# Four ring groups at first, meta indices selected earlier, and the mixer's last products dealt out in steps between the meta rows

## The reference, cut to what matters

```
h = concat(meta_tokens (16), x (512)), padded          # d = 1024
h = h + even_layer(h)      # attention + short conv, then [att, conv] @ w_out
h = h + peer_ffn(h)        # layer 0
h = h + odd_layer(h)       # pooling
h = h + peer_ffn(h)        # layer 1
return h[:, 16:528]

peer_ffn, for a block of tokens:
    hb = rms_norm(h)
    q = hb @ w_query                       # 8 heads x 2 halves x 128
    s = q . sub_keys                       # 128 scores in each of 16 lists
    sv, si = top_k(s, 16)                  # per list
    top_s, top_pos = top_k(sv0[:, None] + sv1[None, :], 16)   # per head
    idx = si0 * 128 + si1 at top_pos       # 128 experts of each token
    gate = softmax(top_s)
    act = gelu(u[idx] . hb)
    y = sum(gate * act * v[idx])           # u, v: 16384 x 1024 per layer
```

## Time and profile before

| | |
|---|---|
| time, median of 3 runs | 3064.41 us (3062.91 to 3065.80) |
| the profiled execution | 3064.01 us, its span 3062.0 us |
| busy share of the span | PE 62%, DVE 68%, ACT 24%, POOL 32% |
| chain that ended last | DMA 57%, PE 18%, DVE 13%, issue 10% |
| moved | 1140.14 MB, mean 372 GB/s; gathers 1090.59 MB |
| loads that wait for the last product (`odd_weights_sync`) | 1540 KB |

### The profile page before, as it was taken

The page is one execution under the profiler, slowest core; times in us unless marked ns, Lnnn a source line. Parts: engine busy times, 40 slices in busy tenths (PEclk is TensorE's granted clock), DMA queues, the critical chain, the costliest instruction groups (busy, mean ns, idle before and its releaser), DMA issues.

```text
span 3062.0 us, 41832 instructions
## 1 busy us (share of the span) xinstructions
PE 1902.6 (62%) x13374; PEld 782.9 (26%) x13374; DVE 2097.0 (68%) x6444; ACT 725.9 (24%) x2829; POOL 994.9 (32%) x1112
## 2 busy tenths in 40 slices
PE   9999866664756466545665566555755566545444
PEld 4765422221222122122222222221222222211111
DVE  2143568887778668676788677866877688755556
ACT  2035112222222222123222222132212322122212
POOL 0000133333443333233333333333333333333332
PEclk9999978776877678767777787777876777666666
DMA  5131389999999999999999999999999999999998
GB/s 195 56 131 55 110 335 418 407 412 420 421 419 413 409 420 408 421 413 416 413 412 411 419 413 413 410 412 421 404 416 410 419 412 407 417 419 417 417 418 336
DMA packets 165492, 1140.14 MB, mean 372 GB/s; under 512 B 18672, under 2 KB 19696, under 8 KB 29856
## 3 DMA queue, kind: packets, MB, share of 16 engines
q0 software_dynamic: 149760, 1090.59, 86.7%
q1 hardware_dynamic: 15520, 46.94, 4.1%
HBM read 1135.30 MB, written 2.10 MB: 371 GB/s over the span
## 4 chain that ended last, share of the span: by engine, by line
DMA 57%; PE 18%; DVE 13%; issue 10%; ACT 1%; POOL 0%; POOLq 0%; DVEq 0%; SPq 0%
DMA ring_early<-in_peer_uv,idx_u 21%; DMA ring_early<-in_peer_vu,idx_u 19%; DMA ring_late<-in_peer_uv,idx_u 10%; DMA ring_late<-in_peer_vu,idx_u 7%; PE psum L1550 3%; PE psum L732 3%; DVE ring_early L1674 3%; PE psum L1105 3%; PE psum L774 2%; PE psum L635 2%; DVE ring_late L1674 2%; PE psum L668 1%; DVE work L1222 1%; PE psum L1083 1%; DVE si L1220 1%
## 5 line engine op out<-in xcount | busy, mean ns | idle before, releaser
L1674 DVE SCALAR_TENSOR_TENSOR ring_early<-ring_early,psum 128x1024 f32<-128x1024 f32 x696 | 847.0, 1217 | 427.4 <-DMA ring_early<-in_peer_vu,idx_u 214.4
L1550 PE MATMUL psum<-ring_early,w_col 128*32 128x256 f32 x5472 | 530.8, 494 | 704.3 <-ACT w_col L1609 647.5
L1674 DVE SCALAR_TENSOR_TENSOR ring_late<-ring_late,psum 128x1024 f32<-128x1024 f32 x344 | 418.8, 1217 | 212.2 <-DMA ring_late<-in_peer_uv,idx_u 141.6
L1471 POOL DMA_INDIRECT ring_early<-in_peer_vu,idx_u x348 | 328.3, 943 | 596.2 <-DVE ring_early L1674 364.3
L1471 POOL DMA_INDIRECT ring_early<-in_peer_uv,idx_u x348 | 326.5, 938 | 591.3 <-DVE ring_early L1674 407.6
L1550 PE MATMUL psum<-ring_late,w_col 128*32 128x256 f32 x2720 | 270.5, 493 | 352.2 <-ACT w_col L1609 326.1
L1550 PEld LDWEIGHTS psum<-ring_early,w_col 128*32 128x32 f32 x5472 | 190.9, 132 | 1078.2 <-issue 754.0
L1609 ACT ACTIVATE w_col<-block_fold,weight 128x32 f32<-128x32 f32 x1024 | 269.3, 313 | 666.9 <-DVE weight L1651 654.3
L1605 ACT ACTIVATE ge<-ga 128x4 f32<-128x4 f32 (+1 forms) x265 | 54.4, 205 | 1321.4 <-DVE ga L1635 1321.4
L1105 PE MATMUL psum<-wq,hbT 128*128 128x512 f32 x512 | 321.5, 717 | 35.9 <-DVE work L1222 34.8
L1471 POOL DMA_INDIRECT ring_late<-in_peer_uv,idx_u x172 | 161.1, 937 | 301.4 <-DVE ring_late L1674 238.7
(11 more groups left out here) (266 smaller groups left out, 2144.1 us busy)
## 6 DMA issues: line engine op xcount, KB each, us to landing
wq<-in_peer_w_query SPq DMA_DIRECT2D x16, 1024.0 KB, 18.7
w_ring<-in_even_w_in SPq DMA_DIRECT2D x5, 2048.0 KB, 7.9
ring_early<-in_peer_vu,idx_u POOLq DMA_INDIRECT x348
ring_early<-in_peer_uv,idx_u POOLq DMA_INDIRECT x348
w_ring<-in_even_w_out SPq DMA_DIRECT2D x1, 4096.0 KB, 14.1
ring_late<-in_peer_vu,idx_u POOLq DMA_INDIRECT x172, 12.9
ring_late<-in_peer_uv,idx_u POOLq DMA_INDIRECT x172, 12.9
hT<-in_x_T SPq DMA_DIRECT2D x4, 528.0 KB, 6.9
```

Of the source, the lines that this page charges most:

```text
L1471: nc.gpsimd.indirect_dma_start(pair_cells(at), None, uv_rows if at.side else vu_rows, bass.IndirectOffsetOnAxis(idx_u[par][:, i:i + 1], 0) ...
L1550: nc.tensor.matmul(block_part(b, n), w_col[:, i % W_SLOTS, :], v_cell(at)[:, part_cols(n)], start=False, stop=last, skip_group_check=True) ...
L1674: nc.vector.scalar_tensor_tensor(out=cell, in0=cell, scalar=1.0, in1=rows, op0=ALU.mult, op1=ALU.mult, accum_out=dot[par][:, i:i + 1]).the ...
```

## The change

- `ORDER` uses the four early groups for the first 40 rows (16 meta rows and 24 of tile 0), and all six from row 40 on; `late_constants` moves on POOL's queue from behind meta row 7 to ahead of row 40.
- TensorE: product 3 moves behind the meta scores, product 4 ahead of the transposes of tile 0; the selection of indices comes before the first query. Products 5 to 9 are cut into nine steps each (`project_step`: the residual or one k) that run as hooks, two behind each meta row at first, and one behind each tile row until row 14. Fill 0 becomes a hook of row 10 and waits for `s_mix` at 5. The wait for all additions moves to tile row 14.
- PSUM banks: products 4 and 6 use bank 3, the rest bank 5; the first query uses bank 5.
- ACT: the meta queries' copies come ahead of tile 0's norm; copies of products 5 to 9 become hooks of rows 5, 9, 13, 21 and 31.
- VectorE: the addition of product 3 and tile 0's norm run inside the meta sort; tile 0's first sort runs in one piece ahead of the dots, its second between the dots of rows 2 to 14.
- The third and fourth queries move from rows 7 and 23 to 13 and 29; the first two of tile 1 from 31 and 47 to 34 and 49; several hooks of tile 0 move by a few rows.

```diff
-META_ORDER = [0, 1, 2, 3, 0, 1, 2, 3, 4, 5, 0, 1, 2, 3, 4, 5]
-EARLY_ROWS = META_ORDER.index(GROUPS_EARLY)
-ORDER = META_ORDER + [n % RING for n in range(2 * XT * TILE_ROWS)]
+EARLY_TILE_ROWS = 24
+EARLY_ROWS = CHUNK + EARLY_TILE_ROWS
+ORDER = ([n % GROUPS_EARLY for n in range(EARLY_ROWS)] +
+         [(GROUPS_EARLY + n) % RING for n in range(2 * XT * TILE_ROWS - EARLY_TILE_ROWS)])
...
         def late_bank(i):
-            return QUERY_BANK if i % 2 else LATE_BANK
+            return psum[:, 3, :] if i in (4, 6) else LATE_BANK
+
+        BANK_FREE = {4: 2, 5: 2, 6: 3, 7: 4, 8: 6, 9: 7}
...
+        PRODUCT_STEPS = 1 + KD
+        PRODUCTS_EARLY = 2 * (CHUNK - 1)
+
+        def project_step(pe, n):
+
+            i, k = 5 + n // PRODUCT_STEPS, n % PRODUCT_STEPS - 1
+            t, half = PROJECTED[i // 2], i % 2
+            c = slice(512 * half, 512 * half + 512)
+            if k < 0:
+                pe.wait_ge(s_mix, BANK_FREE[i])
+                nc.tensor.matmul(late_bank(i), ident[:, :], hres[:, t, c], start=True, stop=False)
+                return
+            ins = nc.tensor.matmul(late_bank(i), catT[:, k, cols_of(t)], w_out_sb[:, k, c], start=False, stop=(k == KD - 1))
+            if k == KD - 1:
+                ins.then_inc(s_proj, 1)
...
             if f:
                 pe.wait_ge(s_dot, CHUNK + RUN * (f - 1))
+            else:
+                pe.wait_ge(s_mix, 5)
...
-        META_QUERIED = (7, 23)
-        FIRST_QUERIED = (31, 47, 63, 79)
+        META_QUERIED = (13, 29)
+        SECOND_SORT = 2
+        FIRST_QUERIED = (34, 49, 64, 79)
...
-            gather_pool(pool, None, 0, range(EARLY_ROWS))
-            late_constants(pool)
-            gather_pool(pool, None, 0, range(EARLY_ROWS, CHUNK))
+            gather_pool(pool, None, 0)
...
+                    if j == 0 and c == EARLY_TILE_ROWS // CHUNK:
+                        rows = EARLY_TILE_ROWS % CHUNK
+                        gather_pool(pool, j, c, range(rows))
+                        late_constants(pool)
+                        gather_pool(pool, j, c, range(rows, CHUNK))
...
-            columns_scalar(act, None, 0, of_chunk(early, 0) + [(12, lambda: piece_exponentials(act, 1)), (12, lambda: stage_gates(act, 1, 1))])
+            columns_scalar(act, None, 0, [(4, first_indices), (5, lambda: piece_exponentials(act, 0)), (5, lambda: take_projected(act, 5)),
+                                          (9, lambda: take_projected(act, 6)), (12, lambda: stage_gates(act, 1, 1)),
+                                          (13, lambda: take_projected(act, 7))] +
+                           of_chunk(early, 0))
...
-            stages = topk_stages(dve, first_piece(1) + 1, 1, P)
-            dots_vector(dve, None, 0,
-                        [(1 + i, stages[i]) for i in range(TOPK_STAGES)] +
-                        [(14, lambda: piece_indices(dve, 1)), (15, lambda: piece_gates(dve, 0))])
+            first = topk_stages(dve, first_piece(1), 0, P)
+            second = topk_stages(dve, first_piece(1) + 1, 1, P)
+            meta_gates_vector(dve)
+            for stage in first:
+                stage()
+            piece_indices(dve, 0)
+            early = ([(SECOND_SORT + i, second[i]) for i in range(TOPK_STAGES)] +
+                     [(SECOND_SORT + TOPK_STAGES, lambda: piece_indices(dve, 1))] +
+                     routing_vector(dve, 1, META_QUERIED, 2, piece_indices))
+            dots_vector(dve, None, 0, of_chunk(early, 0) + [(11, lambda: piece_gates(dve, 0))])
...
             pe.wait_ge(s_setup, SETUP_STEPS)
-            pe.wait_ge(s_mix, 2 * XT)
             open_meta_sum(pe)
-            fill_tensor(pe, 0)
             early = routing_tensor(pe, 1, META_QUERIED, 2)
-            meta_sums_tensor(pe, of_chunk(early, 0) + [(CHUNK + RUN - FILL_AHEAD, lambda: fill_tensor(pe, 1))])
+            products = [(n // 2 if n < 3 * PRODUCT_STEPS else n // 2 + 1, lambda n=n: project_step(pe, n)) for n in range(PRODUCTS_EARLY)]
+            late = ([(n - PRODUCTS_EARLY, lambda n=n: project_step(pe, n)) for n in range(PRODUCTS_EARLY, 4 * PRODUCT_STEPS)] +
+                    [(6 + n, lambda n=n: project_step(pe, 4 * PRODUCT_STEPS + n)) for n in range(PRODUCT_STEPS)])
+            meta_sums_tensor(pe, products + [(10, lambda: fill_tensor(pe, 0)),
+                                             (CHUNK + RUN - FILL_AHEAD, lambda: fill_tensor(pe, 1))] + of_chunk(early, 0))
```

More of the change, by code:

```diff
@@ L1809, in _ @@
             pool.wait_ge(s_meta_rows, 1)
[L1810 to L1812 removed]
+            gather_pool(pool, None, 0)
             def tile(j):
                 for c in range(TILE_CHUNKS):
[L1816 removed]
+                    if j == 0 and c == EARLY_TILE_ROWS // CHUNK:
[3 more added lines that the diff above has]
+                        gather_pool(pool, j, c, range(rows, CHUNK))
+                    else:
+                        gather_pool(pool, j, c)
                     if j == 1 and c < len(WINDOWS):
@@ L1843, in _, with first_indices @@
             stage_u(act, 0, 0)
+            first_query(0)
             take_projected(act, 4)
-            take_projected(act, 5)
-            take_projected(act, 6)
             first_query(1)
-            act.wait_ge(s_piece, 1)
-            stage_u(act, 1, 1)
-            piece_exponentials(act, 0)
-            for i in range(7, 2 * TILES):
-                take_projected(act, i)
+            def first_indices():
+                act.wait_ge(s_piece, 1)
+                stage_u(act, 1, 1)
             def tile(j, hooks, more=True):
@@ L1904, in _ @@
             add_projected(dve, 2)
-            add_projected(dve, 3)
-            norm_vector(dve, 1, P, tile_of(0), 0)
-            for stage in topk_stages(dve, 0, 0, P, meta=True):
+            for i, stage in enumerate(topk_stages(dve, 0, 0, P, meta=True)):
+                if i == 7:
+                    add_projected(dve, 3)
+                if i == 10:
+                    norm_vector(dve, 1, P, tile_of(0), 0)
                 stage()
@@ L1911, in _ @@
             gates_vector(dve, 0, P, 2)
-            stages = topk_stages(dve, first_piece(1), 0, P)
-            for i, stage in enumerate(stages):
-                if i == 4:
-                    meta_gates_vector(dve)
-                if i == TOPK_STAGES - 1:
-                    dve.wait_ge(s_gateT, 1)
-                stage()
-            piece_indices(dve, 0)
             def tile(j, hooks):
@@ L1966, in _ @@
             first_query(0)
-            pe.wait_ge(s_routed, 2)
-            meta_select_tensor(pe, top_i, META_IDX, s_midx)
-            project_tensor(pe, 4)
-            pe.wait_ge(s_gate, 1)
-            meta_select_tensor(pe, soft, META_GATE, s_gateT)
             pe.wait_ge(s_idx, 1)
             pe.wait_ge(s_mgate, 1)
-            project_tensor(pe, 5)
-            project_tensor(pe, 6)
-            pe.wait_ge(s_mix, 4)
             first_query(1)
-            for i in range(7, 2 * TILES):
-                project_tensor(pe, i)
             def tile(j, hooks):
```

37 lines of the change are left out of this document (20 added, 17 removed).

## The result

The changed kernel takes 3077.05 us (median of six, 3070.80 to 3079.31); the kernel before, run beside it, 3063.58 us (median of six, 3062.78 to 3065.80). The ratio is 1.0040, interval 1.0030 to 1.0051: slower by 0.4%, where 3053.0 was forecast. The profiled execution took 3079.31 us around a span of 3077.6 us, so this trace stands 15.6 us behind the span of before, 2 us more than the medians do.

A forecast was written before the change was run, and what follows sets the result against it. The DMA was taken as the bound, with only waste before about 400 us winnable. Row 22 at 441.2 less (423.0 + 3.8 + 3.0) gave 11.4 us off the 3064.4 median: 3053.0, range 3042 to 3062.

The forecast's parts named there:

- What bounds the kernel: DMA is full from 400 us to 3040 us, so only DMA time wasted before about 400 us can count.
- Part 1: Indices earlier: one product fewer ahead of the meta queries, gather 0 at 333.4, 3.3 us earlier, alone worth nothing.
- Part 2: Tile 0's first sort: first dot at 358.5, 2.8 us later; VectorE's 13.38 and 15.83 us waits go.
- Part 3: Dots with the second sort between them: 2.4 us per row on VectorE, inside the DMA's 2.53, so not the bound.
- Part 4: TensorE in the meta rows: first sum 368.8, rows at 2.47 then 3.33 us, gather 22 issued 418.1, landed 423.0.
- the first rival: TensorE keeps up in the meta rows: DMA full from about 361.5, row 22 lands at 410.9, 3041; chance 0.17.
- the third rival: TensorE's clock stays low in its rows 1 to 13: 21 us more, 3074, slower; chance 0.10.
- the sum behind it: From row 22: gain 441.2 less 423.0 landing, 3.8 odd weights and 3.0 for the ring of four, 11.4 us.
- What else moves, at no cost: POOL's memset and wait, SP's odd loads, tile 1's transposes and later sorts move without costing time.
- Four gathers (10 us) are in flight when it opens: Tile 1's transposes at TensorE's row 37 wait for a sort stage at row 45; gathers in flight cover it.
- There is a little room left: Later sorts at a 15-row instead of 16-row distance fit, VectorE's busy share being about 0.9 with a full DMA.
- The second rival: Ring of four starves up to row 40: 2.8 to 2.9 us a row, about 9 us more, 3062, no change; chance 0.15.

The follow-up runs named there:

- e2: Changed kernel with the third query's last step at row 9 instead of 13, so the fourth query's wait reaches 3 rows, not 7: 3067.58 us.
- e12: Changed kernel with only gelu batches of two rows instead of four in rows 0 to 31: 3073.58 us.
- e11: e7 with gelu batches of two rows instead of four in rows 0 to 31: 3054.52 us.
- e7: e6 with TensorE's product steps dealt out more thinly, and ACT's copies of products 7 and 8 moved with them: 3060.21 us.
- e10: Kernel before with four groups for the first 40 rows, shorter waits for the fourth query and tile 1's transposes, and two-row gelu batches in rows 0 to 31: 3073.55 us.
- e13: Kernel before, six groups kept, with only gelu batches of two rows in rows 0 to 31: 3069.12 us.
- e6: Changed kernel with the third query at row 9, tile 1's queries at 31, 47, 63, 79 and its transposes at tile row 24 instead of 21: 3059.24 us.
- e1: Changed kernel with tile 1's queries back at rows 31, 47, 63, 79, 16 rows apart: 3073.14 us.
- e14: Kernel before with only tile 1's queries moved to rows 34, 49, 64, 79, 15 rows apart: 3070.71 us.
- e4: Kernel before with only four groups for the first 40 rows and the POOL wait and clearing moved ahead of row 40: 3083.63 us.
- e15: Changed kernel with third query at 9, tile 1's queries at 31, 47, 63, 79, its transposes at tile row 24, two-row gelu batches in rows 0 to 31: 3054.82 us.

## Why the prediction was wrong, by its own steps

- *What bounds the kernel*: right. The DMA is full behind 680 us at 415 GB/s in after, and every difference between the kernels was made in the gathers ahead of it.
- *Part 1*, gather 0 at 333.4: it went out at 335.12, 1.6 us earlier than before and not 3.3. The mixer ended 0.7 us later in this execution, and from the start of product 4's residual to the transposes behind it were 9.5 us (322.31 to 331.84), where 8.0 was given. Gather 0 alone was worth nothing, as forecast.
- *Part 2*, first dot at 358.5: 360.39, late by 1.9 us, about what gather 0 was late. The waits of 13.38 and 15.83 us on VectorE are gone, as forecast.
- *Part 3*, VectorE not the bound: right.
- *Part 4*, the meta rows: right in its terms up to gather 22, so the first rival (TensorE keeps up) did not come about. First sum forecast at 368.8, measured 370.87; row 0 forecast at 4.5, measured 3.96 (370.87 to 374.83); pitch 2.47 and 3.33 forecast, 2.47 (374.83 to 377.30) and 3.33 (398.86 to 402.19) measured; row 15's sum at 420.54; gather 22 forecast at 418.1, measured 420.42, 2.3 us late, most of it gather 0's delay of 1.7. Its row's dot ran at 425.88, where 423.0 was forecast for the landing. Granted clock 0.65 in 360 to 380, with 15.70 us of idleness ahead of the first sum, and 1.00 from 380 to 420, which is 2.4 GHz: the third rival, a low clock, did not come about, and the slower result has another cause.
- *The step that failed* is the end of part 4 and the sum behind it: "afterwards TensorE has one step a row, 1.6 to 2.0 us, and the DMA is full again", with "Bounds: 0 ... and 18 x 0.25 plus 1.5 for a late stage, 6 us. I take 3." At row 22 the changed kernel's dot was 15.4 us ahead of before, where 18.2 was forecast. Behind row 22 the sum allowed a loss of 6.8 us (3.8 for the weights, 3.0 for the ring), and the dots lost 31.3 by row 200. Rows 22 to 29 of TensorE also hold the fourth query, and its first step waits for a stage seven rows later on VectorE; the sum has no term for that but the 1.5 us for a late stage. In the rows of before such a wait is harmless, because six groups are in use. A ring of four lets a gather go eight rows behind its sum, so a reach of 7 leaves the DMA one or two rows: 10.9 us, shown by shortening that reach (e2). And I had priced the ring by its rate with four in flight, not by the loop of gelu batch, sum and gather, which is eight rows long as well: 4.3 us in the changed kernel (e12), 5.5 with the waits gone (e11 less e7), about 9 as an estimate with four groups in the old order (e10 and e13).
- *"What else moves, at no cost"* held two more. "Four gathers (10 us) are in flight when it opens" at row 37: TensorE stood for 10.64 us, POOL for 10.28, and the DMA moved 336 GB/s in 510 to 520. e6 removed the dip; its price is between 0 and 2.5 us and wasn't settled. "There is a little room left" for the 15-row distance: 5.3 us (e1), and 6.1 in the kernel before (e14). I had asked VectorE's busy share, 18.64 of 20 us in the earlier trace rows; the waits point to the reach instead, 8 for 7. POOL stands for 9.3 to 10.0 us at each of three queries in the changed kernel, for 7.5 to 7.6 in the kernel before. With the shorter waits the DMA moved 409, 415 and 405 GB/s in 560 to 580, 600 to 620 and 640 to 660, with the longer ones 367, 370 and 376.
- The second rival (the ring of four starves, 3062) had the right place and too small a price: it had stages against landing times, not batches and reaches. What the Trainium skill says of a 1 MB transfer (DMA: Bandwidth & Descriptors, Bandwidth, Measured: 341 GB/s) pointed to the same side. The runs give the rate a small share: in e10, with four groups as well, the dots lost only 2.0 us between rows 8 and 40, from 6.0 behind before to 8.0. Of e4's 18.7 us the reaches have 5.1 and the loop about 9; the remaining 4 to 5 are not assigned.

In sum: e15 keeps the whole idea of the change (order on TensorE, steps, ring of four, early indices) and has the four costs removed. It takes 3054.8, 9.8 us under before, where 11.4 was forecast. That the two are so near is in part luck: its row 22 came 20.6 us ahead for the 18.2 forecast, and it lost 9.3 behind it for the 6.8, with pairs that the change does not have.

Two things stay open: the price of the row-37 wait by itself, and the spread of the changed kernel's own runs (3070.8 to 3079.3, nearly three times that of before). The profiles show gather 0 between 331.7 and 336.7 in kernels that have the change's order, and 336.7 to 338.4 in those with the order of before; the mixer's last product starts at moments up to 3.3 us apart (292.4 to 295.7), and that was not followed up.

## What to carry to other kernels

Before a buffer ring is made smaller, list every wait by which an in-order engine stands for a later row of another engine (a score bank, a batch of small arithmetic, a transpose), count its reach in rows, and compare it with the rows that the ring lets a transfer go ahead, at each depth that the ring has. A wait of 7 rows was free with six groups and cost 10.9 us with four, while busy shares said that there was room. And to find out where such a kernel loses, subtract the times of the n-th row in two traces: the gain of the first part and the loss of the second were 22.9 and 38.8 us here, and the totals show only the difference. Take the issues to find the wait and the dots, which stand behind the landing, for its price: at gather 24 the issues showed 7.3 us of lead and the dots 12.1.
